# Moving the activation tiles of a matmul-bound kernel from 64 to 192 bytes beyond a multiple of 256

## The chip, the core and the metric

The kernel runs on one core of one Trainium2 chip. A core has TensorE (PE, with its weight loads shown apart as PEld), VectorE (DVE), ScalarE (ACT), GpSimd (POOL) and SyncE (SP, which here only issues DMAs). SBUF, the on-chip memory, has 128 partitions; every tile has the same address in each partition. The metric is the device time of one execution in microseconds (us): the median of three runs before the change is 1297.44 us, the lowest 1295.89, the highest 1300.59.

## The reference

Two transformer blocks run one after the other on x of 256 rows and 1024 columns (f32). Cut to what matters:

```
# first block
h    = rmsnorm(x, norm_g) * (1 + scale) + shift          # scale, shift, gate from c @ w_ada
proj = h @ w_in                                          # 1024 x 8192
attn = softmax over 3 groups of dilated window attentions of (q, k, v) from proj
y    = sigmoid(g_attn) * ((attn * silu(z_attn)) @ w_attn_br) \
     + sigmoid(g_pool) * ((mixed * silu(z_pool)) @ w_pool_br)
x    = rmsnorm(x + gate * (y @ w_out), final_g)
# second block, layer 0, on x (256 rows) and on ctx (256 rows) together
y = retention_gla_mixer(h, ev_w_in) @ ev_w_out           # chunked gated scans
x = layer_norm(ALPHA * x + g1 * y);  x = layer_norm(ALPHA * x + g2 * (relu(h @ w1) ** 2 @ w2))
# second block, layer 1, on x; keys and values of ctx as well
y = window_attention(rope(q), rope(k), v, k_c, v_c, sink) @ od_w_out
x = layer_norm(ALPHA * x + g1 * y);  x = layer_norm(ALPHA * x + g2 * (relu(h @ w1) ** 2 @ w2))
```

Nearly all of the arithmetic is in the products with weight matrices of 1024 rows: w_in, ev_w_in, ev_w_out, mlp_w1, mlp_w2, od_w_qkv and od_w_out.

## The kernel before

**Weights.** The weight matrices are cut into units of 1024 x 256 (list `units`). SP loads unit u into `raw[u % 6]`; ACT copies it, rounded to the fp32r type that TensorE multiplies in one pass, to `whi[u % 4]` (L1552); DVE writes what the rounding left off, raw minus whi, to `wlo[u % 6]` over the raw tile (L2170). Each activation is kept as such a pair too: `h_hi, h_lo` for the first block's projections, `mz_*` and `at_*` for its two branches, `mg_*` for w_out, `a_hi, a_lo` for the second block's 256 or 512 rows (their halves are also the windowed attention's output and the last MLP's input), and `m_hi, m_lo` for the hidden rows of its MLPs.

**Matmuls.** For each k of the 8 slices of 128 rows three matmuls are issued: hi by hi, lo by hi and hi by lo, each with a weight load (LDWEIGHTS) of its own, which runs while the matmul ahead of it streams. Two orders occur. In the column order (`col_unit` L703, `col_half` L738, and blocks 0 to 3 of each group of an MLP in L1354) the weight slice is stationary and the activation moves past it. In the row order (`row_unit` L722, `row_half` L755, L1258, L1332, L1509, and blocks 4 to 7 in L1354) the activation is stationary and the weights move. In names such as `bank<-whi,m_hi` the moving tile stands first and the stationary one second. A matmul moves 256 columns of one partition's row, 1024 bytes, or 512 columns where 512 rows are done at once; a weight load reads 128 columns, 512 bytes. 24 matmuls with the same target (12 where the weights have 512 rows) fill one half of a PSUM bank.

**Order of the work.** Every engine's instructions are written out by hand in the order in which they run, with semaphores between the engines. TensorE waits for `lo_done` (the unit's wlo), for `free[...]` (its PSUM bank) and, at the start of a stage, for the activation's slices.

**Places in SBUF.** `sb(name, shape, dtype, where)` takes the next bytes of a stack; a tile that belongs to an inner `ExitStack` gives its bytes back when that stack closes, and so tiles of different stages lie over each other. Tiles such as `shift_h`, `shift_a`, `shift_m`, `beside_pT` are never read or written: they only take up room. The slices of 128 or more columns that the products use start at whole multiples of 256 bytes from their tile's start, so a tile's offset from a multiple of 256 is that of each such operand. By the sizes of the tiles these offsets are:

```
tile                              before   after
whi, wlo, raw, xres, graw_a/b          0       0
h_hi, h_lo, mz_hi, mz_lo              64     192
a_hi, a_lo (o_*, n_* are halves)      64     192
m_hi, m_lo                            64     192
at_hi, at_lo, mg_hi, mg_lo           128     192
za, prob, probT, qT, kT, vR, pre     128     192
Y, gy, trB, vv, qd, ki, cres         128       0
q_both, k_hi, k_lo, relu, sq, gtmp   128       0
ident (first tile of C)              128     128
ex, sc                               192     192
```

For one unit each of the two orders reads:

```
for i, (w, x) in enumerate(((wh, hi), (wl, hi), (wh, lo))):        # column order, L703
    mm = nc.tensor.matmul(o, w[:, k, n * P:(n + 1) * P], x[:, k, 0:T], ...)
for j, (w, x) in enumerate(((wh, hi), (wh, lo), (wl, hi))):        # row order, L722
    mm = nc.tensor.matmul(o, x[:, k, m * P:(m + 1) * P], w[:, k, :], ...)
```

Of the kernel before, what the change touches and what calls it, by code (L numbers as in the profile page):

```python
# [9 lines left out]
P = 128  # L10
D = 1024
KT = D // P
# [103 lines left out]
def build(nc, a, out, cst, at, keep, scratch):  # L116
# [3 lines left out]
    with ctx:  # L120
# [7 lines left out]
        def sb(name, shape, dt=f32, where=ctx):  # L128
            return where.enter_context(nc.sbuf_tensor(name, shape, dt))
# [36 lines left out]
        A = ExitStack()  # L166
# [1 line left out]
            graw_a = [sb(f"graw_a{i}", [P, 2, 512], where=e) for i in range(GSA)]  # L168
        strip_b = sb("strip_b", [P, 2, GROUPS, 256], f32r, A)
        sb("beside_strip", [P, GSA * 1024 - 2 * GROUPS * 256], where=A)  # L170
        sb("shift_h", [P, 16], where=A)
        h_hi, h_lo = [sb(n, [P, KT, S], f32r, A) for n in ("h_hi", "h_lo")]
        mz_hi, mz_lo = [sb(n, [P, 4, S], f32r, A) for n in ("mz_hi", "mz_lo")]
        sb("shift_za", [P, 16], where=A)
        za = sb("za", [P, NT, 512], where=A)
        with ExitStack() as e:
            rows_in = sb("rows_in", [P, 2, GROUPS, 256], where=e)
# [39 lines left out]
        T = 2 * S  # L217
        B = ExitStack()
# [1 line left out]
        graw_b = [graw_both[:, i] for i in range(GSB)]  # L220
        lrow = graw_both.rearrange("p i a b -> p i (a b)")
        with ExitStack() as e:
            sb("beside_pT", [P, 16 + KT * T], where=e)
            pT = sb("pT", [P, 2, 4, 2, 2, P], where=e)
        sb("shift_a", [P, 16], where=B)
        a_hi, a_lo = [sb(n, [P, KT, T], f32r, B) for n in ("a_hi", "a_lo")]
        sb("shift_tr", [P, 16], where=B)
        trB = [sb(f"trB{i}", [P, T], where=B) for i in range(2)]
        with ExitStack() as e:
            gy = sb("gy", [P, 4, D], where=e)  # L230
            vv = sb("vv", [P, 4, 512], where=e)
            qd = sb("qd", [P, 4, T], where=e)
            with ExitStack() as e2:
                grow_ev = sb("grow_ev", [P, 2, D], where=e2)
            ki = sb("ki", [P, 4, T], where=e)
            kir = sb("kir", [P, 4, P], where=e)
            with ExitStack() as e2:
                la = sb("la", [P, 4, 512], where=e2)
            kv = sb("kv", [P, 8, DV], where=e)
            sp = [sb(f"sp{i}", [P, 8, DV], where=e) for i in range(2)]  # L240
            dec = sb("dec", [P, 4, 8], where=e)
            lgam = sb("lgam", [P, 12], where=e)
            ssq = sb("ssq", [P, 3, 4, 8], where=e)
            ex = [sb(f"ex{i}", [P, T], where=e) for i in range(2)]
            with ExitStack() as e2:
                lrT = sb("lrT", [2 * RANK + 1, T], where=e2)
                gkw = sb("gkw", [2 * RANK + 1, 2 * RH * DK], where=e2)
            sc = [sb(f"sc{i}", [P, 4, P], where=e) for i in range(2)]
            sc2 = sb("sc2", [P, 4, P], where=e)
# [2769 lines left out]
```

## Time and profile before

| | |
|---|---|
| median of 3 runs | 1297.44 us (1295.89 to 1300.59) |
| profiled execution | 1298.43 us |
| its span, first to last instruction | 1296.5 us |
| mean granted TensorE clock | 0.991 of full speed |
| PE, PEld busy | 1258.7 us (97%), 1163.4 us (90%) |
| DVE, ACT, POOL busy | 880.7, 574.1, 98.0 us |
| chain that ended last | PE 87%, DVE 5%, ACT 3%, DMA 2%, issue 2% |

Outside of the span lie 1.9 us of the profiled execution. A matmul's duration in the profile (about 278 ns) is a modelled one and overlaps the next ones: what a matmul costs in a steady stream is the distance from its start to the start of the next, here called its pitch. The chain of waits shows it: a piece of the chain of n matmuls that lasts t has the pitch t / n.

### The profile page before, as it was taken

How to read it: one execution, taken by the hardware profiler on the slowest of the kernel's cores; microseconds unless marked ns; L12 is line 12 of the kernel's file. 1: busy time of each engine (PE TensorE's matmuls, PEld its weight loads, DVE VectorE, ACT ScalarE, POOL GpSimd, SP SyncE). 2: the span in 40 equal slices, each digit the busy share in tenths (PEclk: the TensorE clock that was granted, in tenths of full speed). 3: DMA queues.
4: the chain of work that ended last, by engine and by line, in shares of the span. 5: the costliest groups of instructions: out<-in, count | busy, mean ns of one | idle time of the engine just before them, and what ended most of it. 6: DMA issues, size and time to landing. Idle time of an engine off the chain costs nothing.

```text
span 1296.5 us, 23842 instructions
## 1 busy us (share of the span) xinstructions
PE 1258.7 (97%) x10165; PEld 1163.4 (90%) x10165; DVE 880.7 (68%) x1371; ACT 574.1 (44%) x900; POOL 98.0 (8%) x145
## 2 busy tenths in 40 slices
PE   6999999999999999999999999999999999999997
PEld 3899999999988777899998898898999878999997
DVE  4567755567555566568677687687787876767666
ACT  4434346554675444536422312313245675544431
POOL 0111111100001111000000011121000000000000
PEclk8999999999999999999999999999999999899999
DMA  9997897455245545033445456476444303555650
GB/s 356 385 312 240 266 247 179 131 176 166 73 129 183 176 155 172 34 104 125 147 142 168 130 172 191 150 245 204 145 160 134 98 2 103 182 174 193 195 163 34
DMA packets 170151, 218.37 MB, mean 168 GB/s; under 512 B 6158, under 2 KB 147861, under 8 KB 169910
## 3 DMA queue, kind: packets, MB, share of 16 engines
q1 hardware_dynamic: 140196, 148.11, 35.0%
q0 software_dynamic: 29152, 67.42, 17.2%
q8 instruction: 81, 1.33, 0.4%
q10 hardware_dynamic: 698, 1.32, 0.3%
q14 instruction: 24, 0.20, 0.0%
HBM read 215.70 MB, written 1.12 MB: 167 GB/s over the span
## 4 chain that ended last, share of the span: by engine, by line
PE 87%; DVE 5%; ACT 3%; DMA 2%; issue 2%; SPq 1%; POOL 0%; DVEq 0%; ACTq 0%
PE bank L1354 31%; PE bank L703 12%; PE bank L722 11%; PE bank L755 7%; PE bank L738 4%; PE bank L1258 2%; PE bank L813 2%; PE bank L904 1%; PE bank L1332 1%; DVE wlo L2170 1%; PE bank L1017 1%; DMA graw_b<-in_w_mod 1%; PE bank L1449 1%; PE bank L1509 1%; PE bank L1182 1%
## 5 line engine op out<-in xcount | busy, mean ns | idle before, releaser
L2170 DVE TENSOR_TENSOR wlo<-raw,whi 128x2048 fp32r<-128x2048 f32 x131 | 297.3, 2274 | 90.6 <-ACT whi L1552 90.4
L1552 ACT ACTIVATE whi<-raw 128x2048 fp32r<-128x2048 f32 x131 | 248.0, 1899 | 181.2 <-PE bank L1354 129.0
L1354 PE MATMUL bank<-a_lo,whi 128*128 128x256 f32 (+1 forms) x688 | 165.3, 312 | 0.0
L1354 PE MATMUL bank<-whi,m_hi 128*128 128x256 f32 x576 | 160.7, 279 | 1.2 <-DVE m_lo L2779 0.8
L1354 PE MATMUL bank<-whi,m_lo 128*128 128x256 f32 x576 | 160.0, 278 | 0.0
L1354 PE MATMUL bank<-wlo,m_hi 128*128 128x256 f32 x576 | 160.0, 278 | 0.0
L1354 PEld LDWEIGHTS bank<-a_lo,whi 128*128 128x128 f32 x688 | 112.1, 188 | 8.8
L1354 PEld LDWEIGHTS bank<-whi,m_hi 128*128 128x128 f32 x576 | 108.5, 188 | 1.9 <-DVE m_lo L2779 1.2
L1354 PEld LDWEIGHTS bank<-whi,m_lo 128*128 128x128 f32 x576 | 108.5, 188 | 0.0
L1354 PEld LDWEIGHTS bank<-wlo,m_hi 128*128 128x128 f32 x576 | 108.1, 188 | 0.1
L703 PE MATMUL bank<-h_hi,whi 128*128 128x256 f32 x336 | 95.0, 283 | 0.0
L703 PE MATMUL bank<-h_lo,whi 128*128 128x256 f32 x336 | 93.6, 279 | 0.0
L703 PE MATMUL bank<-h_hi,wlo 128*128 128x256 f32 x336 | 93.5, 278 | 0.0
L1354 PE MATMUL bank<-a_hi,whi 128*128 128x512 f32 x208 | 82.1, 395 | 0.0
L722 PE MATMUL bank<-whi,a_hi 128*128 128x256 f32 x288 | 81.7, 284 | 0.0
L1354 PE MATMUL bank<-a_hi,wlo 128*128 128x512 f32 x208 | 81.1, 390 | 0.0
L722 PE MATMUL bank<-whi,a_lo 128*128 128x256 f32 x288 | 80.0, 278 | 0.0
L722 PE MATMUL bank<-wlo,a_hi 128*128 128x256 f32 x288 | 80.0, 278 | 0.0
L1354 PE MATMUL bank<-a_lo,wlo 128*128 128x256 f32 x240 | 66.6, 277 | 0.0
L2035 ACT ACTIVATE relu<-bank 128x512 f32<-128x512 f32 x40 | 23.9, 597 | 93.1 <-PE bank L1354 89.9
L703 PEld LDWEIGHTS bank<-h_hi,whi 128*128 128x128 f32 x336 | 63.1, 188 | 1.3 <-issue 0.8
L703 PEld LDWEIGHTS bank<-h_hi,wlo 128*128 128x128 f32 x336 | 63.1, 188 | 0.0
(451 smaller groups left out, 3320.0 us busy)
## 6 DMA issues: line engine op xcount, KB each, us to landing
raw<-in_mlp_w SPq DMA_DIRECT2D x64, 1024.0 KB, 5.2
raw<-in_w_in SPq DMA_DIRECT2D x32, 1024.0 KB, 6.9
graw_b<-in_w_mod POOLq DMA_DIRECT2D x64, 512.0 KB, 4.9
raw<-in_ev_w_in SPq DMA_DIRECT2D x12, 1024.0 KB, 5.1
pre<-in_w_ada SPq DMA_DIRECT2D x16, 512.0 KB, 9.6
graw_a<-in_w_mod POOLq DMA_DIRECT2D x16, 512.0 KB, 6.4
Y<-in_w_mod POOLq DMA_DIRECT2D x16, 512.0 KB, 4.2
raw<-in_od_w_qkv SPq DMA_DIRECT2D x6, 1024.0 KB, 4.9
```

The costliest lines, as they stand in the source:

```text
L703: mm = nc.tensor.matmul(o, w[:, k, n * P:(n + 1) * P], x[:, k, 0:T], start=(k == 0 and i == 0), stop=(k == kt - 1 and i == 2))
L722: mm = nc.tensor.matmul(o, x[:, k, m * P:(m + 1) * P], w[:, k, :], start=(k == 0 and j == 0), stop=(k == kt - 1 and j == 2))
L738: mm = nc.tensor.matmul(o, w[:, k, n * P:(n + 1) * P], x[:, k, c0:c0 + S], start=(k == 0 and i == 0), stop=(k == KT - 1 and i == 2))
L755: mm = nc.tensor.matmul(o, x[:, k, ms], w[:, k, :], start=(k == 0 and j == 0), stop=(k == KT - 1 and j == 2))
L813: mm = nc.tensor.matmul(o[j:j + 32, 0:256], cw[:, 2 * r + kk, :], vslot(q)[:, kk, 256 * half:256 * half + 256], start=(r == 0), stop=(r == 3))
L904: mm = nc.tensor.matmul(bank[u][:, n * UC:(n + 1) * UC], stationary, moving, skip_group_check=True, start=(k == 0 and j == 0 and n == 0), ...
L1017: mm = nc.tensor.matmul(bank[7][:, e * HD:(e + 1) * HD], probT[rc % 2][:, b, :], vR[:, g, kb, h * HD:(h + 1) * HD], start=(blk == 0), stop ...
L1258: mm = nc.tensor.matmul(bank[bk(b)][:, n * UC:(n + 1) * UC], x[:, k, n * P:(n + 1) * P], w[:, k, :], start=(n == 0 and k == 4 and i == 0), ...
L1354: mm = nc.tensor.matmul(o, x, y, start=(k == 0 and i == 0), stop=(k == KT - 1 and i == 2))
L1552: nc.scalar.activation(split_pair(u, kt * cols)[0], landing(u, kt * cols), ACT.Copy).then_inc(hi_done, 1)
L2035: nc.scalar.activation(rel_[:, :], bank[bk(bt)][:, :], ACT.Relu).then_inc(free[bk(bt)], 1)
L2170: nc.vector.tensor_tensor(split_pair(u, n)[1], landing(u, n), bf(whi[u % HI], n), ALU.subtract).then_inc(lo_done, 1)
```

## The change

The unused tile `shift_h` in front of h_hi grows from 16 to 48 floats, which moves h_*, mz_* by 128 bytes; `shift_za` goes, so that the tiles from za on move by 64 bytes. In the second block the 128-byte tile `dec` is moved from the even mixer's inner stack to the place in front of `shift_a`, which moves a_*, m_* and what lies between and behind them by 128 bytes; in the even mixer the tiles behind its old place stay where they were. No instruction is added, removed or moved: on each engine the same instructions stand in the same order with the same tiles, and only addresses differ.

```
-        sb("shift_h", [P, 16], where=A)
+        sb("shift_h", [P, 48], where=A)
         h_hi, h_lo = [sb(n, [P, KT, S], f32r, A) for n in ("h_hi", "h_lo")]
         mz_hi, mz_lo = [sb(n, [P, 4, S], f32r, A) for n in ("mz_hi", "mz_lo")]
-        sb("shift_za", [P, 16], where=A)
         za = sb("za", [P, NT, 512], where=A)
...
         with ExitStack() as e:
-            sb("beside_pT", [P, 16 + KT * T], where=e)
+            sb("beside_pT", [P, 48 + KT * T], where=e)
             pT = sb("pT", [P, 2, 4, 2, 2, P], where=e)
+        dec = sb("dec", [P, 4, 8], where=B)
         sb("shift_a", [P, 16], where=B)
         a_hi, a_lo = [sb(n, [P, KT, T], f32r, B) for n in ("a_hi", "a_lo")]
...
             sp = [sb(f"sp{i}", [P, 8, DV], where=e) for i in range(2)]
-            dec = sb("dec", [P, 4, 8], where=e)
             lgam = sb("lgam", [P, 12], where=e)
```

## Rows read from the trace of the kernel before

**Rows 1.** Page: busy time and share, and the chain that ended last.

```profile
PE 1258.7 (97%) x10165; PEld 1163.4 (90%) x10165; DVE 880.7 (68%) x1371; ACT 574.1 (44%) x900; POOL 98.0 (8%) x145
...
PE 87%; DVE 5%; ACT 3%; DMA 2%; issue 2%; SPq 1%; POOL 0%; DVEq 0%; ACTq 0%
```

**Rows 2.** Chain, h, a and m streams: start us, length us, engine, line, matmuls.

```profile
64.25 16.33 PE bank L703 x144
...
121.81 11.30 PE bank L722 x96
...
140.19 16.96 PE bank L703 x144
...
164.22 10.90 PE bank L722 x96
```

**Rows 3.** Chain, the second block's MLPs and od products, same columns.

```profile
761.84 22.61 PE bank L1354 x192
...
841.78 21.78 PE bank L1354 x192
...
957.06 19.79 PE bank L755 x168
...
1138.28 38.08 PE bank L1354 x336
...
1182.02 39.58 PE bank L1354 x336
...
1227.05 38.08 PE bank L1354 x336
```

**Rows 4.** Chain, w_out with mg_hi and mg_lo, same columns.

```profile
314.35 11.39 PE bank L722 x96
```

**Rows 5.** Chain, matmuls of 512 columns in the first MLP, same columns.

```profile
875.34 21.99 PE bank L1354 x96
```

**Rows 6.** Groups by shape: names, shapes, count | busy us, mean ns | idle before.

```profile
L722 PE MATMUL bank<-whi,mg_lo 128*128 128x256 f32 x48 | 13.5, 281 | 0.0
...
L703 PE MATMUL bank<-at_lo,whi 128*128 128x256 f32 x32 | 9.0, 281 | 0.0
...
L703 PE MATMUL bank<-mz_lo,whi 128*128 128x256 f32 x32 | 8.9, 278 | 0.0
```

**Rows 7.** Groups by shape: the streams that carry the count of matmuls.

```profile
L1354 PE MATMUL bank<-whi,m_lo 128*128 128x256 f32 x576 | 160.0, 278 | 0.0
L1354 PE MATMUL bank<-wlo,m_hi 128*128 128x256 f32 x576 | 160.0, 278 | 0.0
...
L703 PE MATMUL bank<-h_lo,whi 128*128 128x256 f32 x336 | 93.6, 279 | 0.0
...
L1354 PE MATMUL bank<-a_lo,whi 128*128 128x256 f32 x480 | 83.7, 278 | 0.0
...
L1354 PE MATMUL bank<-a_lo,whi 128*128 128x512 f32 x208 | 81.6, 392 | 0.0
L722 PE MATMUL bank<-whi,a_lo 128*128 128x256 f32 x288 | 80.0, 278 | 0.0
```

**Rows 8.** Groups by shape: DVE operations on tiles of several offsets.

```profile
L2607 DVE TENSOR_TENSOR xres<-xres,trB 128x512 f32<-128x512 f32 x24 | 16.6, 692 | 0.8
...
L2486 DVE TENSOR_TENSOR sc<-sc 128x512 f32<-128x512 f32 x8 | 5.5, 692 | 0.3
L2692 DVE TENSOR_TENSOR m_lo<-sq,m_hi 128x512 fp32r<-128x512 f32 x8 | 5.5, 692 | 5.6 <-ACT m_hi L1993 5.6
```

**Rows 9.** Groups by shape: DVE and ACT on the weights.

```profile
L2170 DVE TENSOR_TENSOR wlo<-raw,whi 128x2048 fp32r<-128x2048 f32 x130 | 296.8, 2288 | 90.6 <-ACT whi L1552 90.4
```

More of the change, by code:

```diff
@@ L170, in build @@
         sb("beside_strip", [P, GSA * 1024 - 2 * GROUPS * 256], where=A)
-        sb("shift_h", [P, 16], where=A)
+        sb("shift_h", [P, 48], where=A)
         h_hi, h_lo = [sb(n, [P, KT, S], f32r, A) for n in ("h_hi", "h_lo")]
         mz_hi, mz_lo = [sb(n, [P, 4, S], f32r, A) for n in ("mz_hi", "mz_lo")]
-        sb("shift_za", [P, 16], where=A)
         za = sb("za", [P, NT, 512], where=A)
@@ L222, in build @@
         with ExitStack() as e:
-            sb("beside_pT", [P, 16 + KT * T], where=e)
+            sb("beside_pT", [P, 48 + KT * T], where=e)
             pT = sb("pT", [P, 2, 4, 2, 2, P], where=e)
+        dec = sb("dec", [P, 4, 8], where=B)
         sb("shift_a", [P, 16], where=B)
@@ L240, in build @@
             sp = [sb(f"sp{i}", [P, 8, DV], where=e) for i in range(2)]
-            dec = sb("dec", [P, 4, 8], where=e)
             lgam = sb("lgam", [P, 12], where=e)
```

## The prediction

> **What bounds the kernel now.** I read the page's busy times first, then the chain that ended last. TensorE is busy 97% of the span and carries 87% of the chain; VectorE, at 68%, carries 5% [rows 1]. So the end is set by how closely matmuls follow each other, and a change of addresses counts if it changes that pitch, or if it slows another engine or a transfer so far that TensorE has to wait.
>
> The next view is the chain in order of time, where a piece of n matmuls gives the pitch. Matmuls of 256 columns against the weights run at one of two pitches. Fast: 16.33 us for 144 is 113.4 ns, 10.90 for 96 is 113.5 [rows 2], 21.78 for 192 is 113.4, 38.08 for 336 is 113.3 [rows 3]. Slow: 16.96 for 144 and 11.30 for 96 are 117.8 and 117.7 [rows 2], 22.61 for 192, 19.79 for 168 and 39.58 for 336 are 117.8 [rows 3]. Nothing in the code tells a fast stretch from a slow one: the three pieces of 336 lie in the last MLP, pass through the same kinds of blocks with the same tiles, and go fast, slow, fast. Each piece contains three units in row order and four in column order, and the pitch stays as it was when the order changes. The offsets are the same in all of them, weights at 0 and activations at 64 beyond a multiple of 256.
>
> There is a third pitch. w_out uses mg_hi and mg_lo, at 128, and runs at 11.39 us for 96, which is 118.6 ns [rows 4]; the modelled durations show the same, 281 ns for the mg_lo and at_lo tiles (both at 128) against 278 for mz_lo (at 64), in the same line L703 and with the same number of matmuls [rows 6]. So the distance between the stationary operand that is being loaded and the moving one does matter, if not much: at 128 no stretch is fast.
>
> **The change, part by part.** No instruction is added, removed or moved, so the whole sum is made of pitches and durations that may change.
>
> 1. h, mz, a, m: from 64 to 192. Let d be the moving operand's offset minus the stationary one's. Now d is +64 in column order and -64 in row order. Afterwards it is +192 and -192. Counted modulo 256, +192 is -64 and -192 is +64: the two orders exchange their distances. Both distances stand in the trace already, and both run at 113.3 in the first and third piece of 336 and at 117.8 in the second [rows 3]. If only the distance modulo 256 (or modulo 128, where all four are one) counts, the two pitches stay and the term is 0. How many matmuls are at stake: the groups of 256 columns that rows 7 show are one of three operand pairs each, so m in L1354 is 3 x 576, h in L703 3 x 336, a in L722 3 x 288, a in L1354 480 plus as many again by half (only its lo-by-hi partner, 240, is a separate group), in all some 4,300; with the same kinds in L738, L755, L1258, L1332 and L1509 I take 6,500 as an estimate. Half of them run at each pitch in rows 2 and 3 taken together: 144 + 96 + 192 + 336 + 336 = 1,104 fast, 96 + 144 + 192 + 168 + 336 = 936 slow. The mean is 113.4 + 0.46 x 4.4 = 115.4 ns. The bounds are: all fast, 6,500 x (115.4 - 113.3) = -13.7 us; all slow, 6,500 x (117.8 - 115.4) = +15.6; all at the third pitch, 6,500 x (118.6 - 115.4) = +20.8. I take 0, the value of the geometry that is already there, and keep these ends for the rivals. What share is fast may still change within the same geometry, since a stretch seems to take its pitch from the moment at which it starts after a wait: for one long piece of 336 that changes sides it is 336 x 4.4 ns = 1.5 us, and two such changes either way, 3 us, is what I allow for.
>
> 2. at and mg: from 128 to 192. Their 96 and 192 matmuls (3 x 32, and 3 x 48 in L722 [rows 6] with 3 x 16 in a line of its own) leave the third pitch: 288 x (118.6 - 115.4) = -0.9 us. Bounds: 288 x (118.6 - 113.3) = -1.5 us if all go fast, 0 if they keep it.
>
> 3. Matmuls of 512 columns with a_hi and a_lo, all in column order: 21.99 us for 96 is 229.1 ns [rows 5], which is 2 x 113.3 and 2.5 more. d goes from +64 to -64 modulo 256. I take 0. If they came down to 2 x 113.3, the 3 x 208 of L1354 [rows 7] would give 624 x 2.5 = -1.6 us; if they cost as much more as the slow pitch does to a short one, 624 x 4.4 = +2.7.
>
> 4. VectorE and ScalarE. Operations of 128 x 512 from SBUF to SBUF take 692 ns with trB at 128, with sc at 192 and with m_lo at 64 [rows 8]: three offsets, one duration. The heaviest of all, on raw, whi and wlo [rows 9], keep their addresses. Term 0. They are covered besides, VectorE being idle 32% of the span [rows 1]; 1% on all of its busy time would be 8.8 us, mostly hidden.
>
> 5. Transfers. Only pre, poolM, the tiles of the windowed softmax and a few rows tiles land elsewhere, in steps of 64 or 128 bytes; the 1 MB weight loads land where they did. Term 0.
>
> The sum is -0.9 us on the profiled execution's own 1298.4, so 1297.5. The median of the three runs lies 1.0 lower than that execution, so for a median I say 1296.5. Its own range, from part 1's 3 us, part 2's and part 3's bounds, is 1292 to 1302.
>
> By the Trainium skill the whole difference ought to be absent: its page "TensorE: Matmul & The Clock Gate", section "Step-by-step: what each phase is for", says that TensorE has two independent SBUF read ports and that loading the next weights takes no read bandwidth from the running matmul. By that rule part 2 would be 0 and the time 1297.4. The rows speak against it, with 118.6 ns at d = 128 against at most 117.8 elsewhere, by an amount too small to decide anything here.
>
> **The rivals.**
>
> *All in a bad distance (slower).* If the chip's pattern repeats only after 512 bytes or more, +192 and -192 are distances that the trace does not show in these streams, and may be like 128 or worse. For it: between 64 and 128 the pitch got worse, and the trace holds no case at 192 modulo 512 of this kind. Against it: at and mg have d = +128 in column and -128 in row order, which would be different distances modulo 512 yet show the same 281 ns [rows 6], and +64 and -64 behave alike. The place is every 256-column stream of L703, L722, L738, L755 and L1354; the price is 3.2 ns x 6,500 = 20.8 us at the third pitch, hence 1296.5 + 20.8 + 0.9 = 1318, and 1312 if all just go slow. It decides from a mean of 116.4 ns on, which is 6.5 us more.
>
> *The fast share grows (faster).* At the new distance a stream could always settle at 113.3. For it: the fast pitch exists, so nothing in the work forbids it. Against it: both signs of d have slow stretches now. The time is 1296.5 - 13.7 = 1283; with 512-column matmuls too, 1281.
>
> *The exchange costs a little.* If the sign of d has a say in how often a stream falls into the fast pitch, the exchange helps one order and harms the other. I estimate that two thirds of the 6,500 are in row order (in rows 7 the m and L722 groups, 2,592 of 4,320, are, and L755 adds more), so a shift of a tenth of the share in opposite directions moves 0.1 x 6,500 / 3 x 4.4 ns = 1.0 us: this stays inside the forecast.
>
> *The change does nothing at all*, at and mg included: 1297.4, inside it too.
>
> **How the numbers follow.** Forecast, no change that can be told: 0.64. Slower through a bad distance: 0.21. Faster through a larger fast share: 0.15. A measurement of this kernel can tell about 0.5%, 6.5 us, from no change; the forecast's own range, 1292 to 1302, lies within that, so the same three numbers are the chances of same, slower and faster. The range that is to hold the time 8 times in 10 takes the forecast's own and from each rival the part with a partial effect, down to 1286 (three quarters of the way to all fast) and up to 1311 (all slow, nearly).
>
> **What would show it.** Right: the pieces of the chain in L703, L722 and L1354 again at 113.3 to 113.5 and 117.7 to 117.8 ns, both present; the w_out stretch near 314 us below 118 ns, and mg_lo and at_lo at 278 ns; DVE operations of rows 8 still at 692. Wrong: a single pitch everywhere, or a third one, such as 118.6, on h, a and m. A changed share of fast stretches with the same two pitches would leave the mechanism standing and show only that I mis-sized the share.

## The result, and the profile after

The changed kernel took 1306.39 us (median of 4 runs, 1304.26 to 1307.66), the kernel before 1297.60 (4 runs, 1295.89 to 1300.59). The ratio is 1.006, with a 95% interval of 1.0045 to 1.0076: slower by 0.6%, little but beyond what a measurement of this kernel confuses with no change. The forecast was 1296.5 and no change. The profiled execution took 1306.77 us, with a span of 1305.0 at a mean granted clock of 0.990 (before: 1298.43, 1296.5, 0.991), so 8.5 us of span are to be explained. The clock has a small part in them: in this trace it falls to half once more than in the trace of before, for 3.4 us in the last MLP. The first line below is the kernel before at that place, the second the changed kernel (stretch in us: its length, PE busy and its matmuls, granted clock, DMA share, GB/s):

```profile
1136.90:1141.00 4.10, 4.10 (x38) 1.00 0.37 98
```

```profile
1144.50:1147.90 3.40, 3.40 (x18) 0.50 0.28 53
```

Ahead of it TensorE waits in L1331 for m_lo, 2.6 us from start to start of its matmuls (1.9 before). The 16 matmuls started in that stretch are 213 ns apart instead of 113 to 118, which costs some 1.5 us. The experiment that moves the first block alone has such a stretch too and no loss, so the stretch doesn't account for the change's loss.

The page's busy times and chain by engine, changed kernel, to be read against [rows 1]:

```profile
PE 1266.8 (97%) x10165; PEld 1168.9 (90%) x10165; DVE 881.2 (68%) x1371; ACT 573.9 (44%) x900; POOL 98.0 (8%) x145
...
PE 87%; DVE 5%; ACT 3%; DMA 2%; issue 2%; SPq 1%; POOL 0%; DVEq 0%; ACTq 0%
```

TensorE is busy 8.1 us longer with the same 10,165 matmuls; VectorE gained 0.5, ScalarE lost 0.2, and the shares of the chain are the same. Now the chain in order of time (start us, length us, engine, line, matmuls; line numbers are one lower than before, as one line of the program went). Pieces that answer to [rows 2], [rows 4], [rows 3] and [rows 5]:

```profile
64.82 16.96 PE bank L702 x144
...
123.41 11.30 PE bank L721 x96
...
141.79 16.34 PE bank L702 x144
...
314.78 11.31 PE bank L721 x96
...
765.07 22.62 PE bank L1353 x192
...
846.15 22.62 PE bank L1353 x192
...
880.53 22.41 PE bank L1353 x96
...
1145.82 39.71 PE bank L1353 x336
...
1190.97 38.94 PE bank L1353 x336
...
1235.57 38.73 PE bank L1353 x336
```

Three things stand there. The first block has fast and slow pieces as before. w_out, at 314.78, went from 118.6 to 117.8 ns, as forecast. And in the second block the piece of 192 near 846 went from fast to slow, the one of 96 with 512 columns (880.53) from 229.1 to 233.4 ns, and the pieces of 336 (seven units of 48 matmuls, three in row order and then four in column order) have a new kind of length: 38.73 is neither 336 x 113.3 = 38.07 nor 336 x 117.8 = 39.58. It is 144 x 117.8 + 192 x 113.3 = 38.7: the three units in row order slow, the four in column order fast. 38.94 is the mirror image, 144 x 113.3 + 192 x 117.8 = 38.9, and 39.71 is 38.7 and the 1 us that the half clock costs within it. Counted from start to start, the parts are indeed at 117.8 and 113.4, then 113.3 and 117.8. The two orders no longer go together, and the pitch can change where the order changes, without a longer gap there. It was the same for both orders within each of these pieces before.

The modelled durations say the same more faintly. Groups by shape, changed kernel (names, shapes, count | busy us, mean ns | idle before), against [rows 7], [rows 8] and [rows 9]:

```profile
L2169 DVE TENSOR_TENSOR wlo<-raw,whi 128x2048 fp32r<-128x2048 f32 x130 | 296.9, 2289 | 91.8 <-ACT whi L1551 91.4
...
L1353 PE MATMUL bank<-whi,m_lo 128*128 128x256 f32 x576 | 161.1, 280 | 0.0
...
L1353 PE MATMUL bank<-a_lo,whi 128*128 128x256 f32 x480 | 83.1, 278 | 0.0
...
L1353 PE MATMUL bank<-a_lo,whi 128*128 128x512 f32 x208 | 82.2, 395 | 0.0
...
L721 PE MATMUL bank<-whi,a_lo 128*128 128x256 f32 x288 | 80.6, 280 | 0.0
...
L2691 DVE TENSOR_TENSOR m_lo<-sq,m_hi 128x512 fp32r<-128x512 f32 x8 | 5.5, 693 | 5.6 <-ACT m_hi L1992 5.6
```

In row order (whi,m_lo and whi,a_lo) 278 became 280 ns, in column order (a_lo,whi at 256 columns) it stayed 278 with 0.6 us less in all, at 512 columns 392 became 395. VectorE is unmoved.

Three pieces are a poor sample, so I counted the pitch of every matmul of 128 x 256 in both traces, from the start of one to the start of the next. Nearly all fall at 113 to 114 ns (fast) or at 117 to 119 (slow). In the table, as everywhere from here on, d is the moving operand's offset minus the stationary one's, counted modulo 256, so that 192 is -64; the second block begins at 322 us. Each cell has d, the fast share, the mean pitch in ns, and the count.

| | before | after |
|---|---|---|
| second block, row order | -64, 0.55, 115.41 (3,940) | +64, 0.19, 116.94 (3,954) |
| second block, column order | +64, 0.55, 115.34 (1,219) | -64, 0.83, 114.18 (1,221) |
| first block, row order | -64, 0.56, 115.41 (443) | +64, 0.16, 117.08 (597) |
| first block, column order | +64, 0.33, 116.35 (1,113) | -64, 0.46, 115.79 (1,206) |
| 512 columns | +64, 228.99 (698) | -64, 233.29 (698) |

(After, at and mg are counted in the first block's cells. Without mg its row order after is 0.21 fast, at 116.85 over 441 matmuls.) The sum, as count times change of the mean: row order of the second block 3,950 x 1.53 = +6.0 us, its column order 1,220 x -1.16 = -1.4, the 512 columns 698 x 4.30 = +3.0, the first block 440 x 1.44 = +0.6 and 1,110 x -0.56 = -0.6, and at and mg about -0.5. That is +7.1 of the 8.5 us. The rest lies in the longer gaps between matmuls, which sum to +1.2 us; the half clock gives some 1.5 of it, and the waits make up for the rest.

Each cell is one trace, and a share varies from trace to trace. In the nine later runs that leave the distances of h and mz as they were, the first block's shares run from 0.09 to 0.32 in column order and from 0.40 to 0.51 in row order. A change of 0.1 in one cell therefore says nothing. The second block's row order is clear of that: 0.53 to 0.61 in the four traces that have it at -64, 0.18 to 0.25 in the three that have all of it at +64.

### The profile page after: what moved, and what is told of

The parts are those of the page before. It is cut to its first block, busy times and chain, and to the rows that moved or that the text cites. A ratio compares the mean times of both kernels' runs of the same rounds, so it can differ in the third digit from the quotient of the medians.

```text
span 1305.0 us, 23842 instructions
## 1 busy us (share of the span) xinstructions
PE 1266.8 (97%) x10165; PEld 1168.9 (90%) x10165; DVE 881.2 (68%) x1371; ACT 573.9 (44%) x900; POOL 98.0 (8%) x145
## 4 chain that ended last, share of the span: by engine, by line
PE 87%; DVE 5%; ACT 3%; DMA 2%; issue 2%; SPq 1%; POOL 0%; DVEq 0%; ACTq 0%
PE bank L1353 31%; PE bank L702 12%; PE bank L721 11%; PE bank L754 7%; PE bank L737 4%; PE bank L1257 2%; PE bank L812 1%; PE bank L903 1%; PE bank L1331 1%; DVE wlo L2169 1%; PE bank L1016 1%; PE bank L1448 1%; DMA graw_b<-in_w_mod 1%; PE bank L1508 1%; PE bank L1181 1%
```

## The experiments

The theory after the result, R: what counts is d modulo 256, alike in both orders. -64 is the good sign for 256 columns, in that more streams start fast, and the bad one for 512. Row order has 3.2 times as many matmuls in the second block, so handing it +64 loses. The rivals: A, the activations' own offset counts (192 is worse than 64); period 512, where 192 is a distance unlike -64; O, the first block or its transfers did it; C, the pitches come from contention with other engines.

The edits are shown against the kernel before.

**The second block alone.**

```
-            sb("beside_pT", [P, 16 + KT * T], where=e)
+            sb("beside_pT", [P, 48 + KT * T], where=e)
...
+        dec = sb("dec", [P, 4, 8], where=B)
...
-            dec = sb("dec", [P, 4, 8], where=e)
```

> Only the second block's part of the change: a and m tiles at 192, the first block as before (h, mz at 64, at, mg at 128). Theory R (the distance moving minus stationary operand, modulo 256, sets how often a stream falls into the fast pitch of 113.3 ns; +64 in row order is the bad case): the second block's row-order streams go from over half fast to about a fifth, its 512-column matmuls from 229 to 234 ns, and the time is 4 to 7 us above the kernel before, ratio 1.003 to 1.0055. Theory O (the first block's tiles, or the landing places of its transfers, carry the loss): within 2 us of the kernel before.

Measured: 1307.87 us (4 runs), ratio 1.0068 (1.0049 to 1.0087), more than I had written for R (1.003 to 1.0055). The whole loss is here. Counted, the second block is that of the changed kernel (row order 0.18 fast, column order 0.81, 512 columns 233.29), the first that of before. The chain of this kernel:

```profile
845.31 22.62 PE bank L1354 x192
...
879.70 22.41 PE bank L1354 x96
```

**The first block alone.**

```
-        sb("shift_h", [P, 16], where=A)
+        sb("shift_h", [P, 48], where=A)
...
-        sb("shift_za", [P, 16], where=A)
```

> Only the first block's part of the change: h, mz, at, mg at 192, the second block as before. Theory R: column order gains (about a third to under half fast), row order loses (over half to a sixth), at and mg leave 118.6 ns; the terms cancel within 1 us, 1297 to 1301 us on this chip and ratio 0.999 to 1.001. Theory O (transfers or other tiles of the first block): a loss of 2 us or more.

Measured: 1298.44 us (10 runs), ratio 0.999 (0.9972 to 1.0009). O has fallen from both sides. The first block's row order went to 0.19 fast and its column order to 0.42; there column order is the larger part, and the two cancel. The second block is as before, its chain again with a fast piece of 336:

```profile
1225.75 38.08 PE bank L1353 x336
```

**Activations at 192, weights at 128.** Everything moves up by 128, so the offsets are those of the changed kernel and the distances those of before, but for at and mg, which come to +64 and -64.

```
+        dec = sb("dec", [P, 4, 8])
         whi = [sb(f"whi{i}", [P, KT * UC], f32r) for i in range(HI)]
...
-        sb("shift_za", [P, 16], where=A)
...
-            dec = sb("dec", [P, 4, 8], where=e)
```

> All tiles from whi on are moved by 128 bytes together: weights at 128, h, a, m at 192, so that the distances +64 in column and -64 in row order are those of the kernel before while the activations' own offset is that of the changed kernel. at and mg come to a distance of 64 as well, worth -1 us. Theory R: 1296 to 1298 us, row order again more than half fast, 512-column matmuls at 229 to 230 ns. Theory A (an activation at 192 is bad by itself, wherever the weights are): 1304 to 1308 us, row order one fifth fast, 512 columns at 234 ns.

**Second block's activations left at 64, weights at 128.** The offsets are those of before, the distances of the second block those of the changed kernel.

```
+        dec = sb("dec", [P, 4, 8])
         whi = [sb(f"whi{i}", [P, KT * UC], f32r) for i in range(HI)]
...
-        sb("shift_za", [P, 16], where=A)
...
-            sb("beside_pT", [P, 16 + KT * T], where=e)
+            sb("beside_pT", [P, 48 + KT * T], where=e)
...
-        sb("shift_a", [P, 16], where=B)
+        lgam = sb("lgam", [P, 12], where=B)
+        sb("shift_a", [P, 32], where=B)
...
-        sb("shift_tr", [P, 16], where=B)
+        sb("shift_tr", [P, 8], where=B)
...
-            dec = sb("dec", [P, 4, 8], where=e)
-            lgam = sb("lgam", [P, 12], where=e)
...
-                sb("shift_m", [P, 112], where=e2)
+                sb("shift_m", [P, 120], where=e2)
```

> Weights at 128, the second block's a and m at 64 modulo 256, so that the distance there is -64 in column and +64 in row order, as in the changed kernel, while the activations' own offset is the old one; the first block has its old distances (at and mg at a distance of 64). Theory R: like the kernel with only the second block changed, 1300 to 1304 us, with row order about a fifth fast in the second block and 512 columns at 234 ns. Theory A: 1296 to 1298 us and 229 to 230 ns.

Measured: with activations at 192 and the old distances 1301.53 us (10 runs), ratio 1.0012 (0.9997 to 1.0028); with activations at 64 and the new distances 1308.65 (4 runs), 1.0065 (1.0043 to 1.0088). Both times lie above what R had said (1296 to 1298 and 1300 to 1304 us), though here the kernel before itself took 1299.71. The loss follows the distance, not the offset, and A has fallen. The two chains, first the one with the old distances:

```profile
843.99 21.78 PE bank L1353 x192
...
877.55 22.00 PE bank L1353 x96
```

and then the one with the new:

```profile
846.85 22.62 PE bank L1353 x192
...
881.66 22.41 PE bank L1353 x96
```

Piece by piece the first reads like the kernel before and the second like the changed one. Over the whole second block, row order is 0.59 fast in the first and 0.25 in the second; 512 columns 229.6 and 233.3. Column order is 0.36 fast in the first, at +64, and 0.54 in the second, at -64. The sign acts the same way, but 0.54 is what column order had at +64 in the kernel before: for column order in the full kernel the two signs overlap from trace to trace, and it is row order and the 512 columns that tell them apart. Single streams vary more: in the second run row order with m is 0.10 fast and with a 0.45, where the changed kernel has 0.26 and 0.10 at the same distance.

**Second block at 320.** This is 64 modulo 256 and -192 modulo 512.

```
-            sb("beside_pT", [P, 16 + KT * T], where=e)
+            sb("beside_pT", [P, 80 + KT * T], where=e)
...
-        sb("shift_a", [P, 16], where=B)
+        dec = sb("dec", [P, 4, 8], where=B)
+        lgam = sb("lgam", [P, 12], where=B)
+        sb("shift_a", [P, 32], where=B)
...
```

> a and m at 320, which is 64 modulo 256 but another place modulo 512; weights and first block as before. If the pattern repeats after 256 bytes: the kernel before, 1295 to 1300 us, second-block row order more than half fast, 512 columns at 229 to 230 ns. If it repeats only after 512 or more: another pitch or another share of fast streams, a time outside of 1293 to 1302 us.

Measured: 1298.31 us (10 runs), ratio 0.9986 (0.9969 to 1.0002); row order 0.61 fast, column order 0.49, 512 columns 229.04. It is the kernel before again, so the period is 256, not 512. Its chain:

```profile
878.36 21.99 PE bank L1354 x96
...
1231.11 38.08 PE bank L1354 x336
```

**The streams alone.** A small kernel, in which TensorE is all that works during a stream (VectorE issues one small copy between streams), with weights at 0 and activations of zeros at ten offsets.

```
OFFS = (0, 32, 64, 96, 128, 160, 192, 224, 320, 448)
for r in range(ROUNDS):              # two rounds
    for o in OFFS:
        plan += [("col", o, 3), ("row", o, 3)]   # 3 x 48 matmuls of 256 columns
    for o in wide:                               # 0, 64, 192
        plan += [("wide", o, 4)]                 # 4 x 24 of 512 columns
```

> Leaves out the whole computation: streams of matmuls on zeros, hi by hi, lo by hi, hi by lo, 48 per unit, three units in a row, both orders, activation tiles at 0, 32, 64, 96, 128, 160, 192, 224, 320 and 448 beyond a multiple of 512 with the weights at 0; and 512-column streams at 0, 64, 192. Nothing else runs on the core. Theory R: the pitches 113.3, 117.8 and 118.6 ns appear here too, so that they are TensorE's own two reads and not its neighbours'; row order at offset a behaves as column order at 256 - a; 320 as 64 and 448 as 192; 512 columns 229 ns at 64 and about 233 at 192. Theory C (the slow pitches come from other engines or transfers on SBUF): one pitch, 113.3 ns, at all offsets.

Its chain, where L90 is column order (d is the offset), L98 row order (d is minus the offset) and L105 the 512 columns. In order: column at 0; column and row at 32; column and row at 64; column at 96, at 128 and at 192; row at 192; row at 320; then 512 columns at 0, 64 and 192. Each piece holds about 0.3 us of start besides its matmuls.

```profile
49.32 17.55 PE bank L90 x144
...
84.91 17.09 PE bank L90 x144
102.24 17.32 PE bank L98 x144
119.81 17.24 PE bank L90 x144
137.30 16.63 PE bank L98 x144
154.18 17.55 PE bank L90 x144
...
189.60 17.37 PE bank L90 x144
...
260.24 16.62 PE bank L90 x144
277.11 17.24 PE bank L98 x144
...
347.00 16.62 PE bank L98 x144
...
398.84 22.07 PE bank L105 x96
421.17 22.28 PE bank L105 x96
443.70 22.67 PE bank L105 x96
```

The steady pitches, counted from starts over both rounds:

| d | 0 | +32 | +64 | +96 | 128 | -96 | -64 | -32 |
|---|---|---|---|---|---|---|---|---|
| 256 columns, ns | 120.0 | 116.7 | 117.8 | 120.0 | 118.7 | 118.7 | 113.3 or 117.8 | 118.4 |
| 512 columns, ns | 226.7 | | 228.9 | | | | 233.3 | |

(At -96 one row-order stream ran at 117.3.) All eight streams at +64 are slow, and six of eight at -64 are fast; 320 and 448 do as 64 and 192. With the other engines idle the pitches are those of the full kernel, so C has fallen as the cause of the pitches. It is not excluded from having a say in the shares, which at +64 differ here (none fast) from the full kernel (0.33 to 0.55 before). The page "TensorE: Matmul & The Clock Gate" of the Trainium skill, section "Step-by-step: what each phase is for", gives TensorE two independent read ports, and by "SBUF — State Buffer", section "Who interferes with whom", TensorE shares neither with another engine. No run here speaks against the second; but TensorE's own two operands do act on each other: the same stream takes from 113.3 to 120.0 ns a matmul by their distance alone.

**The other distances in the full kernel.** Three edits put the second block's activations at 32, 96 and 128; for 32:

```
-            sb("beside_pT", [P, 16 + KT * T], where=e)
+            sb("beside_pT", [P, 8 + KT * T], where=e)
...
-        sb("shift_a", [P, 16], where=B)
+        sb("shift_a", [P, 8], where=B)
```

For 96 the two sizes are 24. For 128 beside_pT takes 32 and lgam (48 bytes, in a place of 64) goes in front of shift_a.

> a and m at 32, distance +32 in column and -32 in row order. Theory R says only that this is a distance of its own: if the gap between the two reads counts, half the gap is worse than 64, row order less than half fast or at a third pitch, and the time 1300 to 1320 us. If only the sign counts, row order is more than half fast and the time 1296 to 1301.

> a and m at 96, distance +96 and -96. Between 64 (two pitches) and 128 (118.6 ns, no fast stretch): if the share of fast streams falls with the distance from -64, 1302 to 1315 us; if only the sign counts, 1296 to 1301.

> a and m at 128, distance 128 in both orders, that of at and mg in the kernel before. Theory R: every second-block stream of 256 columns at 118.6 ns as w_out shows, which is 3.2 ns on some 5,150 matmuls, so 16 us above the kernel before, 1313 to 1318 us. If w_out's third pitch has another cause, within 4 us of the kernel before.

Measured, two runs each: 1312.44 us, ratio 1.0105 (1.006 to 1.0151); 1315.12, 1.0126 (1.0097 to 1.0155); 1315.59, 1.013 (1.01 to 1.0159). The row-order means are 118.31 at -32, 118.18 at -96 and 118.78 at 128, with no fast stretch but 1% in column order at 128. The other widths and orders moved as well: column order is at 116.8 ns at +32 and at 119.9 at +96, and 512 columns at 233.3, 233.3 and 232.7 for 32, 96 and 128. So for 512 columns 233.3 is the usual pitch and it is +64, with 229.0, that stands out. The last piece of 336 in the kernels at 32, 96 and 128, one row from each chain:

```profile
1237.32 39.44 PE bank L1354 x336
```

```profile
1241.32 40.12 PE bank L1354 x336
```

```profile
1241.47 39.88 PE bank L1354 x336
```

So 64 is the best of the five offsets tried in the full kernel (32, 64, 96, 128, 192), and my rival of the bad distance had its place and price about right: at 128 it costs 1.3%, only 192 is not such a distance.

**m back to 64, the rest as in the second block alone.**

```
-                sb("shift_m", [P, 112], where=e2)
+                sb("shift_m", [P, 80], where=e2)
```

> The second block as changed, but the hidden rows m_hi and m_lo, which are only ever stationary operands in row order, back at 64. Theory R: their 2,304 matmuls are again more than half fast, 1.6 ns less each, so 3.7 us below the kernel with the whole second block changed: 1302 to 1305 us, ratio to the kernel before 1.0025 to 1.0045; the a streams stay as changed, 512 columns at 233 to 234 ns. Rival: a stream's share of fast pitches is set by what came before it and not by its own distance; then m stays one fifth fast and the time at 1.006 or more.

Measured: 1303.93 us (10 runs), ratio 1.0033 (1.0017 to 1.005), half of the loss of 1.0068. In one trace there are now both signs in row order: m at -64 is 0.44 fast (115.90 ns, 2,260 matmuls), a at +64 is 0.10 fast (117.33, 1,649). The chain:

```profile
849.94 21.78 PE bank L1354 x192
...
883.50 22.41 PE bank L1354 x96
```

m's piece of 192 is fast again, the 512 columns of a are not. The rival of this run, by which m would have stayed one fifth fast, has fallen. But m did not come back to more than half, as I had expected, and its counted gain is 2,260 x 0.7 = 1.6 us (116.6 ns in the run with the second block alone), where the medians say some 4.5. The trace is that of the slowest of the ten runs, at 1309.69 us; the rest of the gain is not shown.

**How often a stream starts fast.** The small kernel again, with two offsets and 128 starts of 24 matmuls, each after a wait on VectorE of varying length.

```
OFFS = (64, 192)
for r in range(32):
    for o in OFFS:
        plan += [("col", o, 1), ("row", o, 1)]   # 24 matmuls each
...
n = 8 + (37 * i) % 256                           # length of VectorE's copy ahead of each
```

> Leaves out the whole computation: 128 short streams of 24 matmuls on zeros, nothing else on the core, each after a wait for VectorE of another length, in turn in column and row order with the activation at 64 and at 192. Theory R with a lottery at the start: at a distance of -64 (row at 64, column at 192) some streams settle at 113.3 and the others at 117.8, and at +64 (column at 64, row at 192) all or nearly all at 117.8. Rival (the fast pitch at -64 is the rule and only disturbance by other work ends it): all of -64 at 113.3.

The chain of this kernel, where L89 is column and L97 row order, for one round: column at 64 (+64), row at 64 (-64), column at 192 (-64), row at 192 (+64).

```profile
34.92 3.11 PE bank L89 x24
38.36 3.01 PE bank L97 x24
41.74 3.00 PE bank L89 x24
44.99 3.10 PE bank L97 x24
```

At -64, 54 of 64 starts were fast (column 32 of 32, row 22 of 32); at +64, 6 of 64 (1 and 5). A stream takes its pitch within the first six matmuls after the start and keeps it. A fast stream doesn't hand its pitch on: row at 192 always follows column at 192, all of whose starts are fast, and is slow in 27 of 32. What decides a start between the two was not found.

**Each stream at its own best distance.** at and mg at 64; n_hi and n_lo, in column order at 256 columns, in a tile of their own at 192; a and m at 64.

```
-        sb("shift_za", [P, 16], where=A)
...
+        with ExitStack() as e:
+            sb("beside_n", [P, 48 + KT * T], where=e)
+            n_both = sb("n_both", [P, KT * T], f32r, e)
...
-            n_hi, n_lo = [flat(a_lo)[:, i * 2048:(i + 1) * 2048]...
+            n_hi, n_lo = [n_both[:, i * 2048:(i + 1) * 2048]...
```

> The kernel before with mz as before and at, mg at 64, and the last MLP's input n_hi, n_lo, which is only a moving operand, at 192 instead of 64; the other a tiles and m stay at 64 (m at 64 modulo 256). Theory R: mg (192 matmuls) from 118.7 to 115.4, at (96) to 116.4, n (768) from 115.4 to 114.2 ns: 0.6 + 0.2 + 0.9 = 1.7 us less than the kernel before, ratio 0.9975 to 0.9995. If at, mg and n do not answer to their distance: ratio 0.9995 to 1.001.

Measured: 1300.36 us (12 runs), ratio 1.0007 (0.9988 to 1.0027). I had expected 0.9975 to 0.9995. n answered, 0.68 fast at 114.83 ns over 775 matmuls. mg left the third pitch, but hardly a stretch of it went fast, though its distance is -64 in row order; I had counted on a mean of 115.4. In the two runs with weights at 128 mg has the same distance and is nearly all fast, at 113.6 ns: four units are too few to average the starts. mg's piece here:

```profile
315.37 11.31 PE bank L726 x96
```

775 x (115.3 - 114.8) and 96 x 0.8 ns are about 0.5 us together, and the interval is 5 us wide. No version here beats the kernel before.

## Why the prediction was wrong

**Part 1, the exchange: the period and the two pitches held, the term of 0 did not.** "The two orders exchange their distances" and "counted modulo 256" are what the runs at 320, at 128 with shifted weights, and of the streams alone show, and the two pitches came back as forecast. What failed is the step "if only the distance modulo 256 (or modulo 128, where all four are one) counts, the two pitches stay and the term is 0". Modulo 128 is wrong: +64 and -64 differ in how often a stream is fast. The rival "the exchange costs a little" named this, and took a shift of a tenth of the share, 1.0 us, from no row. It was 0.36 in the second block's row order, and 0.28 the other way in its column order; by the four cells of the table the term is +6.0 - 1.4 + 0.6 - 0.6 = +4.6 us instead of 0. The estimate of how much was at stake was good (6,715 matmuls counted for 6,500, 0.65 of them in row order for two thirds).

Could it have been read blind? I read three pieces of 336 in [rows 3] whose pitch stayed as the order changed, and concluded that both signs are alike. That is a sample of three. A count over the whole trace of before gives the second block 0.55 and 0.55, which says the same, but its first block 0.33 at +64 and 0.56 at -64. Two of the four cells spoke for a sign, and would have made the loss a case with a chance of its own. The nine later runs bear that out: row order is above column order in the first block of each. How large it is after the exchange they could not say.

**Part 2, at and mg.** Held: they left the third pitch, and mg went from 118.6 [rows 4] to 117.8 ns, the slow pitch and not the mean of the two. About -0.5 us for -0.9.

**Part 3, 512 columns.** I took 0 and named +2.7 us as the end. It was that end: 4.3 ns on each of 698 matmuls (not 624), 3.0 us. The rows of before held no case at -64, and nothing but a habit of middles spoke for 0. Parts 1 and 3 together are 7.6 us of the 8.5.

**Parts 4 and 5.** Held. VectorE 881.2 for 880.7 us, [rows 8] at 692 to 693 ns, [rows 9] within 0.1 us; the chain gives transfers 2% in both.

**The rivals.** The bad distance is real at 32, 96 and 128, and 192 is not one. The larger fast share came true in column order and, by the same rule, turned round in row order.

**The range.** Part 1's 3 us and the bounds of parts 2 and 3, added up, give 1291.3 to 1303.1, a little more than the 1292 to 1302 that I wrote; the time is outside of both. That the wide range, 1286 to 1311, holds it is luck: its upper part was kept for a bad distance, and that isn't what happened.

## What to carry to other kernels

When fp32r matmuls with a weight load each are the bound, as here (no other type was measured), count the pitch from start to start over every stream and split it by the order of the operands: a mean duration and a few pieces of the chain hide a share. Choose SBUF offsets as a distance between the moving and the stationary operand, for the order and the width that most matmuls have. Where an exchange swaps two cases that differ only in sign, do not price it at nothing: weigh each side with its own count.

## What the runs showed of the hardware

- The pitch of 128 x 256 fp32r matmuls with a weight load each runs from 113.3 to 120.0 ns with d modulo 256, with nothing else working. Equal offsets (d = 0) are, with +96, the worst at 256 columns, 120.0, and the best of those tried at 512, 226.7. At 512 columns +64 takes 228.9, and 233.3 was measured at -64, +32 and +96.
- At d = -64 there are two stable pitches, 113.3 and 117.8 ns, chosen at the start of a stream (54 of 64 fast); at +64 nearly always the slow one (58 of 64).
- At a granted clock of 0.50 these matmuls are 213 ns apart, against 113 to 118 at 1.00.
- Left open: what at a start decides between them; and why in the full kernel before 0.33 to 0.55 of the matmuls at +64 are fast, and alone almost none.
